# State space layer: decay logits from prefix sums spread by DMA instead of triangle matmuls

## What is computed

```python
a_cum = jnp.cumsum((dt * a).reshape(b_, nc, SSD_CHUNK, SSD_GROUPS, hpg), axis=2)
seg = a_cum[:, :, :, None] - a_cum[:, :, None, :]
decay = jnp.exp(jnp.where(causal, seg, -jnp.inf))
cb = jnp.einsum('bcqgn,bckgn->bcqkg', cm, bm)
y_diag = jnp.einsum('bcqkg,bcqkgh,bckghp->bcqghp', cb, decay, xdt)
decay_to_end = jnp.exp(a_cum[:, :, -1:] - a_cum)
states = jnp.einsum('bckgn,bckgh,bckghp->bcghpn', bm, decay_to_end, xdt)
y_off = jnp.einsum('bcqgn,bcghpn,bcqgh->bcqghp', cm, s_enter, jnp.exp(a_cum))
```

## Time and profile before

| | us |
|---|---|
| median of 3 runs | 2774.24 (2773.14 to 2776.42) |
| the profiled execution, its own time | 2779.01 |
| span in its profile | 2777.2 |
| SSD stage, four groups, from DVE's first j = 0 | from 375 to about 695 |
| mean granted TensorE clock | 0.995 |

### The profile page before, as it was taken

How to read it: one execution, slowest core, us unless ns; L and a number is a source line. 1 busy time by engine, 2 the same in 40 slices (tenths; PEclk the granted TensorE clock), 3 DMA queues, 4 the chain that set the end, 5 groups by cost and what they waited for, 6 DMA issues and landing times.

```text
span 2777.2 us, 44605 instructions
## 1 busy us (share of the span) xinstructions
PE 2712.6 (98%) x15242; PEld 2340.1 (84%) x15242; DVE 1946.7 (70%) x3076; ACT 1386.8 (50%) x2064; POOL 37.5 (1%) x56
## 2 busy tenths in 40 slices
PE   6999999999999899999999999999999999999998
PEld 5888888888887788888888888888888888888887
DVE  5566678888777667777767665676777576675775
ACT  5544455555555455555454444444554444444444
POOL 0000000000000011000000000000000000000000
PEclk9999999999999999999999999999999999999999
DMA  6655454443674354466555455555555555555553
GB/s 234 211 187 181 157 195 163 151 159 131 221 248 143 106 155 143 150 199 205 183 180 173 171 197 181 175 183 181 177 187 185 193 186 193 187 191 188 190 189 114
DMA packets 91708, 495.72 MB, mean 178 GB/s; under 512 B 8544, under 2 KB 8672, under 8 KB 45296
## 3 DMA queue, kind: packets, MB, share of 16 engines
q1 hardware_dynamic: 88928, 478.18, 50.7%
q0 software_dynamic: 2000, 13.70, 1.3%
q10 hardware_dynamic: 704, 2.83, 0.3%
HBM read 486.29 MB, written 8.39 MB: 178 GB/s over the span
## 4 chain that ended last, share of the span: by engine, by line
PE 88%; DVE 5%; ACT 3%; DVEq 2%; issue 2%; DMA 1%; ACTq 0%; POOLq 0%
PE pj L1513 49%; PE pj L1516 25%; PE pj L1552 3%; PE pj L1548 3%; PE pj L1551 3%; DVE w_lo L769 1%; ACT w_hi L424 1%; PE mx L1557 1%; PE mx L1878 1%; PE mx L1703 0%; DVEq L781 0%; PE mx L1691 0%; PE mx L1814 0%; PE mx L1815 0%; PE mx L1896 0%
## 5 line engine op out<-in xcount | busy, mean ns | idle before, releaser
L769 DVE TENSOR_TENSOR w_lo<-raw,w_hi 128x1024 fp32r<-128x1024 f32 (+1 forms) x1010 | 1134.4, 1129 | 458.2 <-ACT w_hi L424 442.9
L1513 PE MATMUL pj<-hs,w_hi 128*128 128x512 f32 x3888 | 1383.2, 400 | 9.0 <-DVE xT L782 4.7
L424 ACT ACTIVATE w_hi<-raw 128x1024 fp32r<-128x1024 f32 (+1 forms) x1010 | 982.6, 979 | 661.1 <-PE pj L1513 519.7
L1516 PE MATMUL pj<-hs,w_lo 128*128 128x256 f32 x3888 | 1085.2, 279 | 0.0
L1513 PEld LDWEIGHTS pj<-hs,w_hi 128*128 128x128 f32 x3888 | 731.1, 188 | 187.7 <-issue 6.0
L1513 PE MATMUL pj<-ys,w_hi 128*128 128x512 f32 x2368 | 834.3, 398 | 12.0 <-DVE ys L833 4.0
L1516 PEld LDWEIGHTS pj<-hs,w_lo 128*128 128x128 f32 x3888 | 733.6, 189 | 4.8 <-issue 3.4
L1516 PE MATMUL pj<-ys,w_lo 128*128 128x256 f32 x2368 | 662.0, 280 | 0.0
L1513 PEld LDWEIGHTS pj<-ys,w_hi 128*128 128x128 f32 x2368 | 446.1, 188 | 121.3 <-DVE ys L789 4.7
L1516 PEld LDWEIGHTS pj<-ys,w_lo 128*128 128x128 f32 x2368 | 447.4, 189 | 0.0
L429 ACT ACTIVATE half<-pj 128x256 f32<-128x256 f32 x435 | 165.8, 381 | 511.0 <-PE pj L1516 501.7
(11 more groups left out here) (308 smaller groups left out, 1732.3 us busy)
## 6 DMA issues: line engine op xcount, KB each, us to landing
raw<-in_w_up SPq DMA_DIRECT2D x64, 1024.0 KB, 4.7
raw<-in_w_down SPq DMA_DIRECT2D x64, 1024.0 KB, 4.7
raw<-in_w_ssd SPq DMA_DIRECT2D x48, 1024.0 KB, 4.8
raw<-in_w_ret_a SPq DMA_DIRECT2D x48, 1024.0 KB, 4.8
raw<-in_w_ret_b SPq DMA_DIRECT2D x48, 1024.0 KB, 4.8
raw<-in_w_out SPq DMA_DIRECT2D x64, 640.0 KB, 4.0
raw<-in_w_gate SPq DMA_DIRECT2D x32, 1024.0 KB, 4.7
raw<-in_w_mem SPq DMA_DIRECT2D x16, 1024.0 KB, 5.4
```

Of the source, the lines that this page charges most:

```text
L424: A(hi, w, ACT.Copy).then_inc(hi_ready, 1)
L769: TT(lo, w, hi.bitcast(F32), ALU.subtract).then_inc(split_ready, 1)
L1513: ins = mm(pj[:, k], w_hi[:, s + h, u], m, start=opens and t == 0, stop=False)
L1516: ins = mm(pj[:, k, 0:T], w_lo[:, s + h, u], m[:, 0], start=False, stop=closes and t == order[-1])
```

## The change

The sums are made once, for all 32 heads and both chunks. Inside the last-but-two panel of `gate_out`, PE multiplies the steps by `upto` in both orientations (`sums`): once as 64 rows (chunk and head) of 128 query positions, once as 128 key positions of 64 columns; the small matmul for `decay_to_end` moves there too. ACT copies the first result to `cum_out` (in r0, 64x128) and the second to `cum` (128x64), and takes the exponential for `dte` there. POOL stores `cum_out` to HBM (`cum_rows`, 32 KB) behind the spill of x, waits until both have landed, and then loads, for each group, its rows back so that every partition gets them: 4 loads of 128x512 into `em[0]` to `em[3]` (`cum_load`, 256 KB each), and 2 of 64x4x128 into `eqx` (`eq_load`, 128 KB each). `cum_load` of a later group waits for `ydiag` of the group before, `eq_load` for its `ssd_y`. On DVE, `seg(r)` takes the place of `seg_rhs(r)`: for each of 4 heads one tensor_scalar on 128x128, in place, that subtracts the key's sum and caps the result at 0 (above the diagonal too, where the mask of C*B makes it zero). The 16 matmuls L1703, the 16 matmuls L1751 of four groups and DVE's L1111 are gone. ACT's exponentials read SBUF instead of PSUM. The norm's scratch moves from `em` to r0 and r1.

```diff
@@ POOL
             pool.wait_ge(S["x_tile"], 16)
             pool.dma_start(x_spill, xflat).then_inc(S["x_spilled"], 16)
+            pool.wait_ge(S["cum_ready"], 1)
+            pool.dma_start(cum_rows, cum_out).then_inc(S["cum_saved"], 16)
+            pool.wait_ge(S["cum_saved"], 16)
             pool.wait_ge(S["x_spilled"], 16)
+
+            def cum_load(i):
+                for r in range(4):
+                    src = cum_rows[8 * i + 32 * (r // 2) + 4 * (r % 2):][0:4]
+                    pool.dma_start(em[r], src.rearrange("h q -> (h q)").partition_broadcast(P)
+                                   ).then_inc(S["cum_loaded"], 16)
+
+            def eq_load(i):
+                for u in range(2):
+                    src = cum_rows[8 * i + 32:8 * i + 40].rearrange("(n u) q -> u n q", u=2)[u]
+                    pool.dma_start(eqx[64 * u:64 * u + 64].rearrange("p (n q) -> p n q", n=4),
+                                   src.partition_broadcast(64)).then_inc(S["eq_loaded"], 16)
+            cum_load(0)
+            eq_load(0)
+            for i in range(1, GROUPS):
+                pool.wait_ge(S["ydiag_ready"], i * 4)
+                cum_load(i)
+                pool.wait_ge(S["ssd_y"], i * 4)
+                eq_load(i)
@@ ACT, gate_out_body
+                    if i == 1 and j == 2:
+                        act.wait_ge(S["dte_logits"], 1)
+                        A(cum_out, mx[0:64, 2, 0:128], ACT.Copy).then_inc(S["cum_ready"], 1)
+                        A(cum, mx[:, 1, 64:128], ACT.Copy)
+                        A(dte, mx[:, 1, 0:32], ACT.Exp).then_inc(S["dte_ready"], 1)
@@ ACT, ssd_body
-                        A(em[j - 2], mx[:, 1 + j % 2], ACT.Exp).then_inc(S["decay_ready"], 1)
+                        A(em[j - 2], em[j - 2], ACT.Exp).then_inc(S["decay_ready"], 1)
...
-                        act.wait_ge(S["eq_logits"], i * 1 + 1)
-                        A(eqx, mx[:, 2], ACT.Exp).then_inc(S["eq_ready"], 1)
+                        act.wait_ge(S["eq_loaded"], i * 32 + 32)
+                        A(eqx, eqx, ACT.Exp).then_inc(S["eq_ready"], 1)
@@ DVE, ssd_body
-                def seg_rhs(r):
-                    if r >= 2:
-                        dve.wait_ge(S["seg_ready"], i * 4 + r - 1)
-                    TT(rr[r % 2].rearrange("p (h q) -> p h q", h=4),
-                       da[:, r // 2, bass.ds(i * 8 + 4 * (r % 2), 4)].unsqueeze(2).to_broadcast([P, 4, 128]),
-                       upto.unsqueeze(1).to_broadcast([P, 4, 128]), ALU.mult).then_inc(S["seg_rhs"], 1)
+                def seg(r):
+                    if r == 0:
+                        dve.wait_ge(S["cum_loaded"], i * 64 + 64)
+                    for h in range(4):
+                        w = em[r][:, 128 * h:128 * h + 128]
+                        ins = TS(w, w, cum[:, bass.ds(i * 8 + (32 * (r // 2) + 4 * (r % 2) + h), 1)], 0.0,
+                                 ALU.subtract, ALU.min)
+                    ins.then_inc(S["seg_ready"], 1)
...
-                    if j == 5:
-                        dve.wait_ge(S["seg_ready"], i * 4 + 3)
-                        TT(r0.rearrange("p (h d) -> p h d", h=8),
-                           da[:, 1, bass.ds(i * 8, 8)].unsqueeze(2).to_broadcast([P, 8, 64]),
-                           ones[:, 0:64].unsqueeze(1).to_broadcast([P, 8, 64]), ALU.mult).then_inc(S["eq_lhs"], 1)
@@ PE
+            def sums():
+                pe.wait_ge(S["dt_ready"], 1)
+                steps = da.rearrange("p c h -> p (c h)")
+                mm(mx[0:64, 2, 0:128], steps, upto, start=True, stop=True)
+                mm(mx[:, 1, 64:128], upto, steps, start=True, stop=True)
+                mm(mx[:, 1, 0:32], after, da[:, 0], start=True, stop=True).then_inc(S["dte_logits"], 1)
...
-            pe.wait_ge(S["dt_ready"], 1)
-            mm(mx[:, 1, 0:32], after, da[:, 0], start=True, stop=True).then_inc(S["dte_logits"], 1)
...
-                def seg(r):
-                    pe.wait_ge(S["seg_rhs"], i * 4 + r + 1)
-                    if r >= 2:
-                        pe.wait_ge(S["decay_ready"], i * 4 + r - 1)
-                    mm(mx[:, 1 + r % 2], after, rr[r % 2], start=True, stop=True).then_inc(S["seg_ready"], 1)
...
-                    if j == 6:
-                        pe.wait_ge(S["eq_lhs"], i * 1 + 1)
-                        pe.wait_ge(S["decay_ready"], i * 4 + 4)
-                        for n in range(4):
-                            ins = mm(mx[:, 2, 128 * n:128 * n + 128], r0[:, 128 * n:128 * n + 128], upto, start=True,
-                                     stop=True)
-                        ins.then_inc(S["eq_logits"], 1)
```

More of the change, by code:

```diff
@@ L1099, in ssd_body @@
                     if j <= 3:
-                        seg_rhs(j)
+                        seg(j)
                     if 3 <= j <= 8:
@@ L1619, in gate_out_body @@
                     pieces = [(2 * j + u, tiles(ys, 0, 8), 8 * u, True, True, 1) for u in range(2)]
[L1620 removed]
+                    panel("gate_out", i, j, pieces, mid={4: dt_rows} if (i, j) == (0, 0) else
+                          {4: sums} if (i, j) == (1, 1) else {})
             pe.wait_ge(S["y_gate"], 8)
```

19 lines of the change are left out of this document (8 added, 11 removed).

## The result

| | us |
|---|---|
| median of 4 runs, changed | 2790.5 (2789.4 to 2791.5) |
| median of 4 runs, before | 2774.35 (2773.14 to 2776.42) |
| ratio | 1.0056, 95% interval 1.0041 to 1.0071 |
| forecast | 2779.2, range 2769 to 2787 |
| profiled execution: span, own time, clock | 2787.6, 2789.4, 0.991 |

The account below looks back on a forecast made before the run. It took PE to bound the middle of each group, and DVE with ACT the stretch from panel 10 to the next panel 4. Terms +0.7, +4.9 and -0.6 summed to +5.0 on 2774.2: 2779.2 us, range 2769 to 2787.

Parts of the forecast that it names:

- step 6: First group: -0.4 for ACT's split, +0.8 `seg`, -0.9 L1751, +4.9 with the load's +5.4; PE's clock fall priced at 0.
- step 3: Groups 2 to 4: +0.8 on DVE's chain, less 0.07 spare and 0.9 of L1751: -0.2 each, -0.6 in all.
- step 5: First load: DVE waits for store and four loads, last landing in 3.5 us: +5.4 us, bounds +4.6 to +6.2.
- step 4: `sums` inside gate_out: three small matmuls at 0.23 us ahead of the spill of x: +0.7 us; ACT's instructions 0.
- Step 1: Matmuls removed on PE, 17.3 us: L1703 after panels 1 to 4 counts 0, L1751 after panel 6 gives -3.6.
- rival A: PE pays back what the chain of waits says, -16.5 us for removed matmuls: 2763.5 us, chance 0.14.
- DVE's 23.2 us against PE's 0.07 us of slack: Second group, j = 0 to `softmax_scale`: DVE and ACT's chain takes 23.2 us; PE starts transposes 0.07 us after it.
- Step 2: DVE's `seg` for `seg_rhs`: 0.80 us each instead of 0.60, +0.8 a group, bounds +0.3 to +1.9.
- Rival C: `seg` is dearer on DVE, 0.27 us or more per tensor_scalar: +4.4 us, 2783.6 us, chance 0.15.
- Rival B: The store to HBM makes an unhidden round trip before the loads: +2.0 us, 2781.2 us, chance 0.16.
- 3.6 us to spare: First group, panel 2 to transposes: PE gets there at 401.1 us, DVE's results at 404.7, so PE's lower clock is hidden.
- The base: Profiled execution 2779.0 us would take 2784.0; the median, 4.8 us lower, was moved by the same +5.0 to 2779.2.

Follow-up runs that it names:

- a_again: The changed kernel itself, unedited, run again on the chip of the next three runs: 2787.97 us, ratio 1.0048 to the kernel before.
- b_seg_short: Kernel before, with the 16 float32 matmuls L1703 cut from 512 columns to 4: 2775.82 us, ratio 1.0002.
- a_dummy: Changed kernel with 16 matmuls of L1703's shape put back on PE behind panels 1 to 4, results unread: 2787.18 us, ratio 1.0037.
- after: The changed kernel's first profiled trace, no further edit: span 2787.6 us; median of its runs 2790.5, ratio 1.0056 to the kernel before.
- a_late: Changed kernel with `seg` moved on DVE from j = 0 to 3 to j = 5 and 6, exponentials and `mix` later: 2768.12 us, ratio 0.9981.
- x_eq: Changed kernel with the first group's `eq_load` issued only after DVE's last `seg`: 2786.69 us, ratio 1.0037.
- the three x_: Changed kernel, separately: `cum_load` reading spilled x (2788.67 us); first `eq_load` issued after the last `seg` (2786.69); a semaphore for each `cum_load` (2787.51).

## Why the prediction was wrong in size and right in kind

Two things failed. The forecast priced a fall of PE's clock at nothing: in step 6 with a reason ("I price it at 0"), in step 3, behind the waits that it saw coming, without one. The runs show some 4.5 us for it in the first trace of the changed kernel and some 3 in the second. And step 5 took 3.5 us for the landing of the last load, which measured 5.3. That L1703 pays nothing, the reading which the forecast rests on, held.

The mark says +13.5 where the steps said +5.0, and +10.8 in a_again. By pieces:

| piece | forecast | measured | how read | in a_again |
|---|---|---|---|---|
| to the spill's issue (step 4) | +0.7 | +1.6 | 367.86 - 366.29 | +0.2 |
| spill's issue to DVE's start (step 5) | +5.4 | +7.6 | 16.64 - 9.01 | +7.6 |
| DVE's start to the first group's end (step 6) | -0.5 | +1.2 | 80.2 - 79.0 | +0.4 |
| groups 2 to 4 (step 3) | -0.6 | +3.1 | 242.7 - 239.6 | +2.6 |

So only step 5 is missed by the same amount in both traces. The misses of steps 3 and 6 vary with when the clock falls, and what stands against step 4 was for the most part there before `sums`, as is said below.

**Step 1, right.** L1703 counted nothing, against a page that puts PE at 98% and a chain that runs through all of them. b_seg_short (ratio 1.0002) and a_dummy show it from both sides, and rival A is out. What the step left out is that removal can cost: b_seg_short's mark is 5.0 us late, by the clock. L1751 gave 0.7 a group where 0.9 stood. The reading that carried this was DVE's 23.2 us against PE's 0.07 us of slack; the chain of waits hid the other chain.

**Step 2, right.** A `seg` costs 0.79 (0.80), and the stretch to `softmax_scale` 23.95 (24.0). The line by shape, over 64 of them:

```profile
L1116 DVE TENSOR_SCALAR xT<-xT,gen x64: 279/282/293, 384.5 to 640.3; 128x128 f32<-128x128 f32 x64
```

282 ns against 285 by slope. Rival C is out.

**Step 4, right.** Three small matmuls at 0.23 were to cost 0.7. PE by time there:

```profile
349.63 0.27 PE L1545 MATMUL pj<-ys,w_lo 128*128 128x256 f32 x1
349.83 0.43 PE L1650 MATMUL mx<-con,small 128*64 128x128 f32 x2
350.19 0.44 PE L1651 MATMUL mx<-small,con 128*128 128x64 f32 x2
350.46 0.36 PE L1652 MATMUL mx<-small,con 128*128 128x32 f32 x2
350.66 0.47 PE L1542 MATMUL pj<-ys,w_hi 128*128 128x512 f32 x1
350.98 0.28 PE L1545 MATMUL pj<-ys,w_lo 128*128 128x256 f32 x1
```

From L1545 to L1545 it is 1.35, so 1.0 above the pitch on PE. Of the spill's 1.6 us, 0.9 was there before `sums`: the L1545 at 349.63 has its like in the kernel before at 348.77,

```profile
348.77 0.28 PE L1516 MATMUL pj<-ys,w_lo 128*128 128x256 f32 x1
```

and from it to the spill's issue it is 18.23 us after and 17.52 before, +0.7 as forecast. Over all traces it is 18.2 to 18.5 in the nine with `sums` there and 17.2 to 17.5 in the five without; the means differ by 1.0. What comes ahead is the same program in all fourteen and ends anywhere from 348.2 to 349.7 us. Why is open; the granted clock from 333 to 341 us doesn't explain it (0.57 in after, 0.79 in a_late, and both come there at 349.6).

**Step 5, mis-sized by 2.2 us.** The store was a small miss: from the spill's issue to the first load's it is 9.53 us (377.39 - 367.86), where to DVE's start it had been 9.01 (375.30 - 366.29), so it costs 0.5 (forecast 0.3). The 3.5 us for the last load was the big one. It took 5.3, because `eq_load` stood right behind it (1.0 by x_eq), and because four loads of 256 KB at once aren't one of 192 KB; the first of them did land in 3.5, and the last in 4.3 without `eq_load`. I had taken a duration of one DMA for the last of a burst. The upper bound, 4.3 beside weights, was too low for the same reason, and it lengthened the wait on PE to 9.64 us. The Trainium skill, page "DMA: Bandwidth & Descriptors", section "Anatomy of one DMA — SWDGE (gpsimd) path", gives 2.0 us plus bytes over 436 GB/s for each DMA, by which such a load would take 2.6 us, an estimate; the trace has 3.5 for the first and 5.3 for the last, and the trace decides. What that section says of the fixed cost, that most of it is the wait for the target memory to confirm the write, no run here separates. Rival B had the right place (DVE's start after 382.5) but the wrong part: the loads, not the store.

**Step 6, wrong in its zero.** "3.6 us to spare" held PE's chain and DVE's apart. In fact DVE's half also waits for ACT and through it for PE's panels. From 384 to 410 us, with PE at half clock to 391.7, DVE waited 3.7 us for ACT and ACT 2.9 for PE; from 466 to 490, in the second group, it was 2.6 and 0.4. From DVE's start to the transposes it took 25.6 us where 24.1 was forecast (23.7 before, +0.8, -0.4). No run holds the clock up through that stall, but the length of the fall varies. In the six traces with this order on DVE (after, a_again, a_dummy and the three x_) PE had the lower clock for 2.9 to 5.1 us after it went on, and from DVE's start to the transposes it is 24.7 to 25.8 us. Less half of the time at the lower clock, that is 23.2 or 23.3 in all six. So the clock sets this stretch, by comparison of traces and not by an edit.

**Step 3, wrong by what a wait triggers; the largest miss.** The forecast named PE's waits of 3 to 4 us and saw them as free. They came (3.7 us), and the time was indeed DVE's: the third group, whose clock holds, takes 79.9 us as before. But in two of the three groups the clock fell behind them in the stretch where PE sets the time, 1.5 us each. a_dummy shows that it takes these waits, and b_seg_short that it takes nothing else of the change. The other 0.6 of the miss are L1751's 0.7 instead of 0.9 and roundings. The Trainium skill, page "TensorE: Matmul & The Clock Gate", section "HAM oscillation — how this bites in real kernels", describes a loop whose DMA waits of 3 to 5 us put the clock down every time. This trace agrees only in kind: shorter waits, of 1.1 and 1.7 us in the second group and of 1.0 and 1.7 in the fourth, went ahead of a fall, and waits of 1.3 and 1.7 in the third did not.

**The base.** I moved the median by the profiled sum. The profiled execution of the kernel before lay 4.8 above its median and that of the changed kernel 1.1 below its own; 5 us of that sort is what the identical stretch behind the mark shows from trace to trace. By the medians the loss is 16.1, by a_again's ratio 13.3, by the mark 13.5 and, in a_again, 10.8. Which of these is nearest isn't settled. All of them lie well above +5.0.

**Where the expected gain went.** Of 17.3 us of matmuls, 13.8 stood under DVE's chain and only turned into waits. 3 us were won with L1751. Against that stand, in the first trace, 7.6 us for a load that DVE waits for at the start, 3 for `seg`, 1.6 up to the spill (0.7 of them `sums`) and some 4.5 for a lower clock (1.5 in the first group, 3 in the others).

## What to carry to other kernels

- Before an operation of the busiest engine is taken away, look in each stretch for a second chain that ends within its slack; the chain of waits shows only the last one. Where it ended 0.07 us earlier, removal gave nothing, and the replacement on the other engine cost in full. With its work moved one stretch later, the change gave 2.3 us a group (77.6 against 79.9).
- A wait for the last of a burst of DMAs was longer than the row of a single one (5.3 us against 3.5 for the first of the burst): price it with all that is queued beside it, what stands behind it included. A semaphore for each piece let DVE start 3.5 us earlier, though the medians don't show the gain. Better, put the first use behind other work: a_late without the wait was 7 to 9.5 us faster than with it.
- An idle time that is hidden may not be free on PE: the clock can fall behind it in a stretch that isn't hidden. Where in a run it falls varies from trace to trace of one kernel, so price it as a range (here 0 to 1.5 us a group) and don't leave it at nothing.

## What was not expected of the hardware

- A float32 matmul of 4 columns takes 253 ns where 128 columns take 275, beside a weight load of 192. Cutting columns below 128 saved nothing there (the group of four cost PE 0.90 us either way); cutting 512 to 4 saved 0.64 of 0.86 us.
- The granted clock fell for 3.4 us behind waits of 1.1 and 1.7 us on PE with 0.8 us of work between them, in two groups of three with such waits, in each of five traces. b_seg_short shows it behind a wait of 1.7 us alone.
- Two DMAs queued by POOL one behind the other, the spill of 2 MB and the store of 32 KB, cost together 0.5 us more than the spill alone.
- The same 2080 us of program, in one kernel after the other, took 2078.5 to 2083.8 us.
